# First block's in-projection as three rounded products per slot

## The reference, cut to what matters

```
proj = h @ w_in[i]                       # (256, 1024) @ (1024, 1952)
sb_q, sb_k, sb_v, q_lat, kv_lat, k_rope = split(proj, [512, 1024, 1536, 1792, 1920])
o_sb  = stick_breaking_attention(sb_q, sb_k, sb_v)        # 8 heads of 64
q     = rms_norm(q_lat, g_q_lat) @ w_q_up ; kv = rms_norm(kv_lat, g_kv_lat) @ w_kv_up
k_rope = apply_rope(k_rope, cos, sin)                     # 32 wide, shared by 8 heads
o_mla = mla_attention(q_nope, rope(q_rope), k_nope, k_rope, v_mla)
```

## Time and profile before

| | before |
|---|---|
| median of 3 launches | 994.34 us (993.92 to 997.03) |
| the profiled launch | 995.91 us |
| its span in the profile, first to last instruction | 994.1 us |
| TensorE busy, share of the span | 813.6 us, 82% |
| VectorE / ScalarE / GpSimd busy | 331.9 / 309.9 / 143.9 us |
| mean granted TensorE clock | 0.928 of full speed |
| moved by DMA | 297.93 MB, mean 300 GB/s |

### The profile page before, as it was taken

The page is one execution under the profiler, slowest core; times in us unless marked ns, Lnnn a source line. Parts: engine busy times, 40 slices in busy tenths (PEclk is TensorE's granted clock), DMA queues, the critical chain, the costliest instruction groups (busy, mean ns, idle before and its releaser), DMA issues.

```text
span 994.1 us, 12347 instructions
## 1 busy us (share of the span) xinstructions
PE 813.6 (82%) x5144; PEld 528.1 (53%) x5144; DVE 331.9 (33%) x700; ACT 309.9 (31%) x621; POOL 143.9 (14%) x153
## 2 busy tenths in 40 slices
PE   7998879999999999999889998767666775665854
PEld 5856447899997886687768542213112221221212
DVE  3306465667676545559531310001000000100001
ACT  2316355666665556645541300000100000000001
POOL 0011013344443005135400000000000000000000
PEclk9999989999999999999989999879989688889779
DMA  9932964454553566733809799999999999999994
GB/s 359 428 113 82 396 273 169 157 183 170 183 197 109 220 216 218 294 143 116 307 1 404 263 398 396 428 431 426 429 428 427 429 428 428 428 427 427 430 428 201
DMA packets 23677, 297.93 MB, mean 300 GB/s; under 512 B 2752, under 2 KB 3008, under 8 KB 5440
## 3 DMA queue, kind: packets, MB, share of 16 engines
q1 hardware_dynamic: 23616, 297.09, 74.1%
HBM read 296.03 MB, written 1.05 MB: 299 GB/s over the span
## 4 chain that ended last, share of the span: by engine, by line
PE 53%; DMA 33%; DVE 6%; ACT 5%; POOL 1%; issue 1%; SPq 0%; DVEq 0%; POOLq 0%
PE ps L186 53%; DMA ring<-in_exps 32%; ACT ar L200 1%; POOL ar L217 1%; DVE ar L206 1%; ACT yT L200 1%; DVE fr L206 1%; ACT ar L197 1%; DMA ring<-in_win 1%; DVE yT L214 0%; ACT fr L197 0%; DVE misc L596 0%; ACT sq L200 0%; DVE yT L206 0%; PE ps L619 0%
## 5 line engine op out<-in xcount | busy, mean ns | idle before, releaser
L186 PE MATMUL ps<-ring,sq 128*32 128x512 f32 x976 | 138.1, 703 | 71.0 <-DMA ring<-in_exps 70.7
L186 PE MATMUL ps<-ring,ar 128*32 128x512 f32 (+3 forms) x792 | 106.7, 629 | 51.6 <-DMA ring<-in_exps 44.5
L186 PE MATMUL ps<-fr 128*128 128x256 f32 (+1 forms) x852 | 144.9, 325 | 4.7 <-DVE fr L206 4.3
L186 PEld LDWEIGHTS ps<-fr 128*128 128x128 f32 x852 | 124.9, 190 | 20.3 <-DVE fr L206 4.1
L186 PEld LDWEIGHTS ps<-ring,sq 128*32 128x32 f32 x976 | 29.7, 119 | 169.1 <-DMA ring<-in_exps 113.3
L186 PE MATMUL ps<-hT,ring 128*128 128x256 f32 (+2 forms) x416 | 93.3, 385 | 6.8 <-DMA ring<-in_win 6.8
L206 DVE TENSOR_TENSOR ar<-ar,ps 128x512 f32<-128x512 f32 x9 | 6.2, 688 | 253.7 <-PE ps L186 253.7
L186 PEld LDWEIGHTS ps<-hT,ring 128*128 128x128 f32 (+2 forms) x416 | 78.1, 189 | 20.8 <-DMA ring<-in_win 6.8
L186 PEld LDWEIGHTS ps<-ring,ar 128*32 128x32 f32 (+1 forms) x792 | 28.0, 121 | 112.4 <-DMA ring<-in_exps 69.7
L186 PE MATMUL ps<-ar 128*128 128x512 f32 (+9 forms) x320 | 72.8, 462 | 14.8 <-DVE ar L206 8.9
L206 DVE TENSOR_TENSOR fr<-ring,fr 128x512 fp32r<-128x512 f32 x79 | 65.1, 842 | 44.2 <-ACT fr L197 44.0
(11 more groups left out here) (194 smaller groups left out, 931.8 us busy)
## 6 DMA issues: line engine op xcount, KB each, us to landing
ring<-in_exps SPq DMA_DIRECT2D x90, 2048.0 KB, 30.7
ring<-in_modw SPq DMA_DIRECT2D x12, 2048.0 KB, 8.2
ring<-in_wup SPq DMA_DIRECT2D x11, 2048.0 KB, 8.8
ring<-in_win SPq DMA_DIRECT2D x5, 2048.0 KB, 9.2
ring<-in_wdown SPq DMA_DIRECT2D x5, 2048.0 KB, 8.3
ar<-in_exps SPq DMA_DIRECT2D x3, 2048.0 KB, 12.4
ring<-in_wo SPq DMA_DIRECT2D x2, 2048.0 KB, 10.1
ring<-in_wgate SPq DMA_DIRECT2D x2, 2048.0 KB, 8.5
```

Source lines behind the costliest of these rows:

```text
L186: return pe(lambda e: e.matmul(o, l, r, start=start, stop=stop, skip_group_check=True), *waits, inc=inc)
```

## The change

The products of all four slots, except those of the first two tiles of slot 0 and of the rope key, become three float32r products of rounded parts and rests. `split` moves up; `in_parts` makes the parts of one tile of weights, in one of four buffers for slots 0 and 1, and one of two for slots 3 and 2; `in_products` issues the three products for each place, tile after tile (k outer), so that all places of a slot end together. The parts of `hT` are made once, at the start, and kept in the memory of `qm` and `km`. The rope key's copy into `km` is therefore issued behind the values' products. The squares of x, the Silu and the tables of angles come later in the program than before.

```diff
--- before.py
+++ after.py
@@ -306,13 +306,64 @@
         th = []
         for k in range(8):
             th.append(v_ts(tile(hT, k), tile(xT, k), col("g_pre_mix", k), None, ALU.mult, None, d_x[k // 4], d_g))
-        tsq = [a_fn(sq[:, 1024 * i:1024 * i + 1024], xT[:, 1024 * i:1024 * i + 1024], ACT.Square, d_x[i]) for i in range(2)]
-        t_silu = a_fn(silu_c, col("c", 0, 8), ACT.Silu, d_cols)
 
         def tiles_of(w, m, nt=8, ncol=512, width=128, src=None, toks=None, at=0):
             src, toks = (hT, th) if src is None else (src, toks)
             return [(w.ap(k * ncol + m, width), tile(src, k, at), toks[k]) for k in range(nt)]
 
+
+        rx0 = ar[:, rxo:rxo + S]
+        b = 0
+
+        def x_stats():
+            return wide_factor(0, [(tile(sq, k), tsq[k // 4]) for k in range(8)], 0, 1024, rx0)
+
+        IX, IW = (7680, 9728), [3072, 4096, 5120, 6144]
+        i_n, i_free = [0], {}
+
+        def split(src, hi, lo, low, *waits):
+            t = a_copy(hi, src, *waits)
+            return low(lo, src, hi.bitcast(F32), ALU.subtract, t)
+
+        def in_parts(src, low, *waits):
+            i = IW[i_n[0] % len(IW)]
+            i_n[0] += 1
+            n = src.shape[1]
+            h, l = fr[:, i:i + n], fr[:, i + 512:i + 512 + n]
+            return i, h, l, split(src, h, l, low, i_free.get(i), *waits)
+
+        def in_products(k, parts, places):
+            i, wh, wl, t_w = parts
+            xh, xl = (tile(fr, k, o) for o in IX)
+            for m, (o, width) in enumerate(places):
+                c = slice(128 * m, 128 * m + width)
+                mm(o, wh[:, c], xh, k == 0 and m % 2 == 0, False, t_w, t_in[k])
+                mm(o, wh[:, c], xl, False, False)
+                t = mm(o, wl[:, c], xh, False, k == 7, inc=int(m == len(places) - 1))
+            i_free[i] = t
+            return t
+
+        t_in, first = [], {}
+
+        def first_parts(k):
+            first[k] = in_parts(ring[:, 512 * k:512 * k + 512], p_tt if k % 2 else v_tt, d_w0[k // 2])
+
+        for k in range(8):
+            t_in.append(split(tile(hT, k), tile(fr, k, IX[0]), tile(fr, k, IX[1]), v_tt, th[k]))
+            if 2 <= k < 6:
+                first_parts(k)
+        tsq = [a_fn(sq[:, 1024 * i:1024 * i + 1024], xT[:, 1024 * i:1024 * i + 1024], ACT.Square, d_x[i]) for i in range(2)]
+        for k in range(8):
+            if k < 2:
+                for m in range(4):
+                    t = mm(bank(4 + m // 2, (m % 2) * S, (m % 2) * S + S), ring[:, 512 * k + 128 * m:512 * k + 128 * m + 128], tile(hT, k),
+                           k == 0 and m % 2 == 0, k == 7, d_w0[k // 2], th[k], inc=int(m == 3))
+            else:
+                t = in_products(k, first[k], [(bank(4 + m // 2, (m % 2) * S, (m % 2) * S + S), 128) for m in range(4)])
+                if k < 4:
+                    first_parts(k + 4)
+        freed[0] = t1 = t2 = t_first = t
+        t_silu = a_fn(silu_c, col("c", 0, 8), ACT.Silu, d_cols)
 
         R, R2, RS = slice(64, 96), slice(64, 128), slice(96, 128)
         pf, kk, an = ar[R2, rt:rt + S], ar[R2, rt + S:rt + 2 * S], ar[R2, rt + 2 * S:rt + 3 * S]
@@ -334,18 +385,7 @@
             t = v_ts(o, o, -3.1415925, None, ALU.max, None, t)
             t_tab.append(t)
 
-
-        rx0 = ar[:, rxo:rxo + S]
-        b = 0
-
-        def x_stats():
-            return wide_factor(0, [(tile(sq, k), tsq[k // 4]) for k in range(8)], 0, 1024, rx0)
-
-        for k in range(8):
-            for m in range(4):
-                t = mm(bank(4 + m // 2, (m % 2) * S, (m % 2) * S + S), ring[:, 512 * k + 128 * m:512 * k + 128 * m + 128], tile(hT, k),
-                       k == 0 and m % 2 == 0, k == 7, d_w0[k // 2], th[k], inc=int(m == 3))
-        freed[0] = t1 = t2 = t
+        t1 = t2 = t_first
         t_rx = x_stats()
         t_q = []
         for j, t in enumerate((t1, t2)):
@@ -367,14 +407,15 @@
 
         w = stream("win", 1)
         t_k = []
+        for k in range(8):
+            p = in_parts(w.ap(512 * k, 512), p_tt if k % 4 == 3 else v_tt, w.ready)
+            t = in_products(k, p, [(bank(6 + m // 2, (m % 2) * S, (m % 2) * S + S), 128) for m in range(4)])
+        w.free(t)
         for j in range(2):
             b = 6 + j
-            chain(bank(b, 0, S), tiles_of(w, 256 * j), w.ready)
-            t = chain(bank(b, S, 512), tiles_of(w, 256 * j + 128))
             o = ar[:, kT + 512 * j:kT + 512 * (j + 1)]
             read[b] = v_tt(by(o, S), by(bank(b), S), wide(rx0, 2), ALU.mult, t, t_rx)
             t_k.append(read[b])
-        w.free(t)
         rcol = misc[:, 4:6]
         for j in range(2):
             t = mm(ps[:, 1, j:j + 1], rx0[:, 128 * j:128 * j + 128], ones[:, 0:1], True, True, t_rx, inc=j)
@@ -485,10 +526,14 @@
 
         w = stream("win", 3, 8 * 448)
         bq, bk, bkr = 4, 5, 6
-        chain(bank(bq, 0, S), tiles_of(w, 0, ncol=448), w.ready, read[bq])
-        t1 = chain(bank(bq, S, 512), tiles_of(w, 128, ncol=448))
-        chain(bank(bk, 0, S), tiles_of(w, 256, ncol=448), read[bk])
-        t2 = chain(ps[R2, bkr, 0:S], tiles_of(w, 384, ncol=448, width=64), read[bkr])
+        IW = [11776, 15360]
+        lat_places = [(bank(bq, 0, S), 128), (bank(bq, S, 512), 128), (bank(bk, 0, S), 128)]
+        lat_parts = [in_parts(w.ap(448 * k, 384), v_tt, w.ready, t_tab, read[bq], read[bk]) for k in range(2)]
+        for k in range(8):
+            t1 = t2 = in_products(k, lat_parts[k], lat_places)
+            if k < 6:
+                lat_parts.append(in_parts(w.ap(448 * (k + 2), 384), v_tt, w.ready))
+        t2 = chain(ps[R2, bkr, 0:S], tiles_of(w, 384, ncol=448, width=64), w.ready, read[bkr])
         w.free(t2)
         lat = yT
         read[bq] = t1 = v_tt(by(lat[:, 0:512], S), by(bank(bq), S), wide(rx0, 2), ALU.mult, t1, t_rx)
@@ -500,20 +545,30 @@
         read[bkr] = tb
         t_kr = v_tt(kr, kr, kr2, ALU.add, ta, tb)
         t_kr = v_tt(kr, kr, rx0[R, :], ALU.mult, t_kr)
+
+        sb_weights(0)
+        sb_weights(1)
+
+
+        w = stream("win", 2)
+        t_v = []
+        v_parts = [in_parts(w.ap(512 * k, 512), v_tt, w.ready) for k in range(2)]
+        t_vp = {}
+        for k in range(8):
+            i, wh, wl, t_w = v_parts[k]
+            for j in range(2):
+                xh, xl = (fr[:, o + S * k + 128 * j:o + S * k + 128 * j + 128] for o in IX)
+                mm(bank(7 - j), xh, wh, k == 0, False, t_w, t_in[k], read[7 - j])
+                mm(bank(7 - j), xl, wh, False, False)
+                i_free[i] = t_vp[j] = mm(bank(7 - j), xh, wl, False, k == 7, inc=1)
+            if k < 6:
+                v_parts.append(in_parts(w.ap(512 * (k + 2), 512), v_tt, w.ready))
         t_kmr = pool(lambda e: e.tensor_copy(
             ar[R, km:km + 2048].rearrange("p (h t) -> p h t", t=S),
-            ar[R, rt:rt + S].rearrange("p (o t) -> p o t", o=1).broadcast_to([32, 8, S])), t_kr)
-
-        sb_weights(0)
-        sb_weights(1)
-
-
-        w = stream("win", 2)
-        t_v = []
+            ar[R, rt:rt + S].rearrange("p (o t) -> p o t", o=1).broadcast_to([32, 8, S])), t_kr, t_vp[1])
         for j in range(2):
             b = 7 - j
-            t = chain(bank(b), [(hT[:, k * S + 128 * j:k * S + 128 * (j + 1)], w.ap(k * 512, 512), th[k]) for k in range(8)],
-                      w.ready, read[b])
+            t = t_vp[j]
             read[b] = a_copy(ar[:, vS + 512 * j:vS + 512 * (j + 1)], bank(b), t, t_rc, scale=rcol[:, j:j + 1])
             t_v.append(read[b])
         w.free(t)
@@ -663,10 +718,6 @@
 
         OX, OW = (0, 2048), [4096, 5120] + [7680 + 1024 * k for k in range(6)]
         o_n, o_free, wo, th, w_o = [0], [None] * 8, {}, [None] * 8, []
-
-        def split(src, hi, lo, low, *waits):
-            t = a_copy(hi, src, *waits)
-            return low(lo, src, hi.bitcast(F32), ALU.subtract, t)
 
         def out_low(k, t, low, *waits):
             hi, lo = (tile(fr, k, o) for o in OX)
```

More of the change, by code:

```diff
@@ L502, in build @@
         t_kr = v_tt(kr, kr, rx0[R, :], ALU.mult, t_kr)
-        t_kmr = pool(lambda e: e.tensor_copy(
-            ar[R, km:km + 2048].rearrange("p (h t) -> p h t", t=S),
-            ar[R, rt:rt + S].rearrange("p (o t) -> p o t", o=1).broadcast_to([32, 8, S])), t_kr)
         sb_weights(0)
@@ L512, in build @@
         t_v = []
+        v_parts = [in_parts(w.ap(512 * k, 512), v_tt, w.ready) for k in range(2)]
[9 more added lines that the diff above has]
+                v_parts.append(in_parts(w.ap(512 * (k + 2), 512), v_tt, w.ready))
+        t_kmr = pool(lambda e: e.tensor_copy(
+            ar[R, km:km + 2048].rearrange("p (h t) -> p h t", t=S),
+            ar[R, rt:rt + S].rearrange("p (o t) -> p o t", o=1).broadcast_to([32, 8, S])), t_kr, t_vp[1])
         for j in range(2):
             b = 7 - j
-            t = chain(bank(b), [(hT[:, k * S + 128 * j:k * S + 128 * (j + 1)], w.ap(k * 512, 512), th[k]) for k in range(8)],
-                      w.ready, read[b])
+            t = t_vp[j]
```

## The result

The changed kernel takes 1013.73 us (median of 4 launches, 1012.92 to 1014.99) where the kernel before takes 995.68 (median of 4, 993.92 to 998.83): ratio 1.0177, 95% interval 1.0150 to 1.0204, slower by 1.5 to 2.0%. The forecast was +13.35 us, 1007.7, with a range up to 1014, so the measured time lies in the range by only 0.3 us.

The account below looks back on a forecast made before the run. DMA sets the end, but its loads wait for slots TensorE frees, so early TensorE time counts. Waits, products and eviction sum to +6.85 and the clock to +6.5: +13.35 on 994.34 gives 1007.7 us, range 998 to 1014.

Parts of the forecast that it names:

- The sign at the values' end: Values' products end at about 84 to 87 us instead of 72.8, with the same shift at 588 us.
- slot 0: In-projection slot 0 in three products ends at 21.6 us where it was 22.53: -0.9 us.
- slot 1, wait, products and clock: First copy waits behind norm work and table loads, 19.6 us between slot ends against 16.1: +3.5; lower clock +2.45.
- late eviction: Slot 1's banks end together, so two 0.69 us evictions run one behind the other before the scores: +0.7.
- slot 3 with clock: TensorE idle 6.0 us behind ScalarE's score work, 18.2 us against 14.15: +4.05; lower clock +2.45.
- slot 2 with clock: 2.45 us idle behind the second Exp, eight tiles 11.0 us where 13.9: -0.5; lower clock +1.6.
- The waits: First products wait for parts: 8.1 us behind slot 0's end, idle 6.0 before slot 3, 2.45 before slot 2.
- The clock: Half clock behind TensorE's idle times: 2.45 us per long gap, 1.6 for the short one, +6.5 in all.
- Rival 1: In-projection slots: idle times are there but the granted clock stays at 1.00; +6.85, 1001.2 us; chance 0.12.
- the pace of slots 3 and 2: Product time at full clock: 8.7 us for slot 3's 72 instructions, 11.0 us for slot 2's eight tiles.
- Rival 2: Expert-weight loads take the in-projection's loss back, so the end does not move: 994.3 us; chance 0.05.
- Rival 3: ScalarE reaches the copies during the preceding slot, so parts are ready ahead: -8.8, 985.5 us; chance 0.11.

Follow-up runs that it names:

- early1: The changed kernel with slot 1's first four parts made right behind slot 0's products, their rests on GpSimd; ratio 1.0122 to the kernel before.
- early: The changed kernel with first parts of slots 1, 3 and 2 made ahead and more buffers for slots 3 and 2; ratio 0.9972 to the kernel before.
- warm: The changed kernel with throwaway native products filling TensorE's idle time before slots 1, 3 and 2; ratio 1.0122 to the kernel before.
- only3: The changed kernel with only slot 3 in three products, the other slots put back to native; ratio 1.0061 to the kernel before.

## Why the prediction was right

The direction, the place and the mechanism held, and the size was 4 to 5 us short. That 1013.73 us still lies under the upper end of the range, 1014, is in part luck: that end was meant for three us of clock behind each gap and GpSimd holding VectorE, and the clock in fact cost less than forecast. The sign at the values' end was missed: 84 to 87 us were named, 89.2 came. Its terms against the trace:

| term | forecast | measured |
|---|---|---|
| slot 0 | -0.9 | -0.1 |
| slot 1, wait, products and clock | +3.5 + 2.45 | +5.8 |
| late eviction | +0.7 | +0.6 |
| slot 3 with clock | +4.05 + 2.45 | +7.5 |
| slot 2 with clock | -0.5 + 1.6 | +2.5 |
| sum | +13.35 | +16.4 |

**The waits** were read from the queue order and came out to a tenth: 8.06 us from slot 0's end to slot 1's first product (forecast 8.1), 5.85 us ahead of slot 3 (6.0), 2.39 ahead of slot 2 (2.45). early1 and early show that they are waits of order, since the same operations in another place of the program take them away, but for 0.7 to 1.6 us inside slot 1 (and early has more buffers as well).

**The clock** was put at 6.5 us and is 5.5 to 5.8 by warm. Rival 1 (the clock stays up) is refuted; its 1001.2 would have been too low even then, for warm, which has just that, is 11 to 12 us over the kernel before.

**The mis-sized term** is the pace of slots 3 and 2: 8.7 and 11.0 us in the forecast, 10.05 and 12.37 with the clock up (warm). That is 2.7 us, against 3.0 that were missing at the values' end; the smaller differences (slot 0 +0.8, slot 1's products +0.3, the clock -0.7, the waits -0.2) nearly cancel. About half of the 2.7 is the two buffers. With five buffers slot 3 takes 9.35 us from its first product to the rope key's (9.98 in warm by the same measure), and with four slot 2 takes 11.17 (the kernel with slot 0 native and all first parts ahead). I allowed 0.15 us for handing over from engine to engine per tile; the ring of free, copy, rest and product goes through three hand-overs, and each pair of slot 2 took 3.1 us, not 2.8. For slot 3 the forecast's own figures, 1.2 us against 1.08, already said that two buffers are not quite enough. That the hand-overs make the difference is worked out, not tested by itself.

Most of the other half is the price of a float32r instruction. At 512 columns the prediction took 0.213 us as an upper bound from 86.5 / 406, and reckoned with 0.218. It is no upper bound: among the 406 are 32 instructions of 128 columns, 16 of 256 and 4 of one. The groups of twelve in the same stretch of the kernel before start 2.72 us apart, 0.227 us each, which is also what slot 2 has with four buffers:

```profile
321.93 2.88 PE L186 MATMUL ps<-fr_h,fr 128*128 128x512 f32 x12
324.65 2.88 PE L186 MATMUL ps<-fr 128*128 128x512 f32 x12
```

So slot 2's saving was 3.0 us at full pace and not 3.5. At 256 columns the new slots ran at 0.121 to 0.126 us an instruction at full clock, instead of 0.120. The N / 2.4 + 2.5 ns that the prediction quotes is in the same section of the Trainium skill ("TensorE: Matmul & The Clock Gate", Back-to-back issue gap) the gap of a matmul by itself, without the loading of weights, so these rows do not contradict it. In slot 0 VectorE and GpSimd held each other, for which the sum had half a us; the first three-product matmul started at 13.62 instead of 13.0.

**What lies behind the stage.** The shift of 16.4 us at the values' end is 17.3 at 161 us, 19.8 at 208 and 18.7 at 607. 2.5 of that come in one stretch, the first 104 instructions of the up-projection, which took 12.54 us at a clock of 1.00 in the kernel before and here

```profile
193.49:207.00 13.51, 13.51 (x92) 0.79 0.01 1
```

15.0 us. In the traces of the eleven experiments that stretch takes 12.5 us twice (only3, early1) and 14.9 to 15.2 nine times. It goes with no edit that I made. In the kernel before, in the changed one and in every experiment the stretch follows an idle time of TensorE of 1.57 or 1.58 us:

```profile
176.16 3.11 PE L186 MATMUL ps<-fr 128*128 128x256 f32 x24 [1.58 <-DVE fr L206]
...
193.49 5.46 PE L186 MATMUL ps<-fr 128*128 128x256 f32 x24 [1.57 <-DVE fr L206]
```

The first row is the kernel before, at a clock of 1.00, the second the changed one, at 0.50 up to 199 us. So the same idle time is followed now by the one level and now by the other; what tips it is open. The same happens behind the values: the kernel with slot 0 alone had 0.50 from 76 us on behind idle times of 1.30 and 0.96 us, where the kernel before, with the same idle times, had 1.00. A quarter of a per cent between two single launches can come from the up-projection's stretch alone.

**Rival 2** (the loads take the loss back) is refuted by the 18.6 us of the span. **Rival 3** (parts ready ahead) was not this kernel, but its condition was named right: once the parts are ahead of the slots the three-product form wins, 3.0 us (0.30%, interval 0.14 to 0.46%) and 5.4 us (0.54%, interval 0.33 to 0.75%) in the two kernels with slot 0 native, of the 8.8 it gave. At the values' end both are 5.2 to 5.3 us ahead. What is missing is slot 0's 1.8 us, native in both, and the pace.

## What to carry to other kernels

A faster form that needs operands made by another engine is priced at its first tile: look up where that engine's queue stands when the stage begins, add copy and subtraction, and compare with the saving. Put the first parts ahead of whatever the queue would do first, as many as cover that work, and check whom the engines that make them slow down. Take an instruction's price from the distance between groups of one shape, not from a mean over a stretch with several shapes. Here a wait on TensorE cost 1.5 us (the gap of 2.4 us) to 2.1 us (the gaps of 5.8) more for the clock behind it, so a gap of 5.8 us was worth 8.

## What the runs showed of the hardware

A float32r instruction of 128 x 128 weights with 256 columns is 0.120 us at full clock, a little over half of a native instruction's 0.218; with 512 columns 0.227 (2.72 us per 12 instructions, in the kernel before and in the kernels with four buffers). So three rounded products win 17% at 256 columns and 22% at 512. An idle time of 2.39 us was followed by the lower clock, as was one of 2.0 us in the kernel before; behind the 1.60 us in early1 the clock stayed at 1.00. The length of the idle time alone does not decide it: behind the same 1.57 us ahead of the up-projection it stayed at 1.00 in three traces and fell to 0.50 in ten. Products whose result is thrown away, put into the three waits, kept it up, and that alone was worth 5.5 us by the ratio and 5.8 in the trace.
